# Expert loop: the order of SiLU, gated activations and weight splits

## The chip, the cores and the metric

The kernel runs on one core of one Trainium2 chip. The metric is the device time of one execution in microseconds. Of three executions of the kernel before, the median is 1717.73 us (1715.55 to 1718.81).

## The reference, cut to what matters

The program is one layer of a hybrid backbone: adaLN modulation, a projection, a bidirectional mLSTM and a Fourier group, an output projection, and then a mixture of experts, with float32 throughout. The change touches only the mixture of experts. Each of 1024 tokens goes to 8 of 64 experts; the 8192 assignments are sorted by expert and padded to blocks of 128 rows. For each block:

```python
def expert_block(args):
    xblk, e = args
    g, u = jnp.split(xblk @ w_expert_gu[e], 2, axis=-1)
    return (jax.nn.silu(g) * u) @ w_expert_down[e]
yb = lax.map(expert_block, (xb, block_e)).reshape(n_rows, d)
routed = jax.ops.segment_sum(yb * row_w[:, None].astype(yb.dtype), row_tok, num_segments=n_tok)
```

A block's input is 128 x 1024, the gate-up weights 1024 x 512 (2 MB), the down weights 256 x 1024 (1 MB).

## The kernel before, in words

Five engines run programs of their own and meet at semaphores. The expert loop begins near 670 us and ends near 1662 us; it works on 104 blocks here, two per iteration of the hardware loop, one call of `step` per block on each engine.

A float32 product is made of three fast products: each operand is split in a high part, a rounded copy in a special float32 form, and a low part, the rest. So every weight chunk (128 x 1024; an expert has four gate-up chunks 0 to 3 and two down chunks 4 and 5) is copied by ScalarE (`w_high`, recorded at L742 with all its copies) and then subtracted by VectorE (`w_low`, L2098). ScalarE counts `hi_split`, VectorE `lo_split`. The same is done with the block's transposed rows (`x_high`, `x_low`; L742, L2087) and with its hidden activations (`h_high`, `h_low`; L742, L2091).

TensorE does in step b: eight transposes of block b+1 (L1430), two transposes of the gated activations of block b-1 (`h_transposes`, L1451), the 24 gate-up matmuls of block b (L1443 to L1445), and the 12 down matmuls of block b-1 (L1465 to L1467). The gate-up matmuls wait for one weight chunk every six matmuls (`lo_split`), and the transposes of L1451 wait for `m_hx`, the gated activations.

ScalarE does in step b, in order: `y_evac` (copies the result of block b-2 from PSUM to one of two buffers; it waits until the scatter that last read this buffer is complete), `h_high`, `x_high`, then, if block b has a new expert, that expert's down chunks 4 and 5; then, if block b+1 has a new expert, a wait for its gate-up weights (`gu_ready`) and chunks 0 and 1; then `silu` of block b (L1010; it waits for the gate-up matmuls of block b), and last chunks 2 and 3. VectorE follows the same order: `h_low`, `x_low`, low halves 4 and 5, low halves 0 and 1, `h_rows` (L2105: gated activations, silu(g) * u * row weight), low halves 2 and 3.

SP loads raw weights into two buffers: the gate-up part of expert e (L536) once the low halves of chunks 0 to 3 of expert e-2 are done (`lo_split`), the down part (L539) once chunks 4 and 5 are done. L573 announces landed gate-up weights to ScalarE. GpSimd gathers rows of a later block (index copy L684, gather L687) once `x_low` of an earlier one is done (`m_xb`), and behind that adds a result to the output rows with a scatter (L698); each scatter waits for the one before it.

Of the kernel before, what the change touches and what calls it, by code (L numbers as in the profile page):

```python
# [121 lines left out]
def build(nc, a, out):  # L122

    ctx = ExitStack()
    with ctx:
# [64 lines left out]
        def bank(i):  # L190
            return psum[:, 512 * i:512 * i + 512]
# [145 lines left out]
        def cols(t, o, n):  # L337
            return t[:, o:o + n] if isinstance(o, int) else t[:, bass.ds(o, n)]
# [401 lines left out]
        def _(act):  # L740
            def copy(o, i):
                return act.activation(o, i, ACT.Copy)  # L742
# [108 lines left out]
            def gate_rows(step):  # L851
                if step == 0:
                    act.wait_ge(S("front_dve"), RF_READY)
                    act.activation(Rl, Rf, ACT.Abs).then_inc(S("rl_step"), 1)
                elif step == 1:
                    act.wait_ge(S("rl_step"), 1)
                    act.activation(Rl, Rl, ACT.Exp, scale=-1.0).then_inc(S("rl_step"), 1)
                elif step == 2:
                    act.wait_ge(S("rl_step"), 2)
                    act.activation(Rl, Rl, ACT.Ln, bias=1.0).then_inc(S("rl_step"), 1)  # L860
                else:
                    act.wait_ge(S("front_dve"), W_READY)
                    col_exp(row(1)[64:100], Rw)
                    act.wait_ge(S("front_dve"), E_READY)
                    act.wait_ge(S("rows_exp"), 2)
                    col_exp(row(2)[0:36], Re)
                    act.wait_ge(S("front_dve"), I_READY)
                    act.activation(Ri, Ri, ACT.Exp).then_inc(S("rows_exp"), 1)
# [74 lines left out]
            def w_high(par, chunks):  # L943

                for c in chunks:
                    copy(cols(wsplit, (1 - par) * (2 * WE) + 1024 * c, 1024), cols(raw, (1 - par) * WE + 1024 * c, 1024)).then_inc(S("hi_split"), 1)
# [44 lines left out]
            def x_high(b, p):  # L991

                act.wait_ge(S("m_xt"), b + 1)
                if isinstance(b, int) and b == 1:
                    copy(xTh[p], psY).then_inc(S("m_xh"), 1)
                else:
                    copy(xTh[p], psum[:, 0:1024]).then_inc(S("m_xh"), 1)

            def h_high(b):
                act.wait_ge(S("m_ht"), b + 1)  # L1000
                copy(hTh, bank(7)[:, 0:2 * P]).then_inc(S("m_hh"), 1)

            def y_evac(b, p):
                act.wait_ge(S("block_done"), b + 2)
                act.wait_ge(S(f"added{p}"), 8 * (b - p) + 16)
                copy(yB[:, p], psY).then_inc(S("m_y"), 1)

            def silu(b, p):
                act.wait_ge(S("m_gu"), b + 1)
                act.activation(sg[:, p], bank(3 + p)[:, 0:DE], ACT.Silu).then_inc(S("m_sg"), 1)  # L1010
# [8 lines left out]
            def step(b, p, here, following):  # L1019

                if here is not None:
                    y_evac(b - 2, p)
                h_high(b - 1)
                x_high(b + 1, 1 - p)
                if here is None:
                    act.wait_ge(S("dn_ready"), 2)
                    w_high(1, range(4, 6))
                else:
                    with act.If_ne(act.to_reg(here[0]), 0):
                        act.wait_ge(S("dn_ready"), here[1] + 2)  # L1030
                        act.sem_inc(S("passed"), 1)
                        w_high(1 - (here[1] & 1), range(4, 6))
                first, par1 = following[0], 1 - (following[1] & 1)
                with act.If_ne(act.to_reg(first), 0):
                    act.wait_ge(S("gu_ready"), following[1] + 2)
                    act.sem_inc(S("passed"), 1)
                    w_high(par1, range(2))
                silu(b, p)
                with act.If_ne(act.to_reg(first), 0):
                    w_high(par1, range(2, 4))  # L1040

            def word(b):
                return word_of(act, b)

            step(1, 1, None, fields(word(1)))
            act.wait_ge(S("table_ready"), 2)
            for i in range(2):
                act.wait_ge(S(f"acc_out{i}"), 64)
            rest = act.value_load(pairs_rest[0:1, 0:1], min_val=NE // 2 - 1, max_val=MAXB // 2 - 1)
            with act.Fori(0, rest) as i:  # L1050
                one, two, three = pair_of(act, i)[0:3]
                step(2 * i + 2, 0, one, two)
                step(2 * i + 3, 1, two, three)
# [487 lines left out]
        def _(dve):  # L1541
# [460 lines left out]
            expert, first, ordinal, more_come = trows  # L2002
# [77 lines left out]
            def x_low(b, p, col):  # L2080

                dve.wait_ge(S("m_xh"), b + 1)
                dve.tensor_copy(gcol[:, p:p + 1], xg[:, p, D:XW][:, bass.ds(col, 1)])
                if isinstance(b, int) and b == 1:
                    tt(xTl[p], psY, xTh[p].bitcast(F32), ALU.subtract).then_inc(S("m_xb"), 1)
                else:
                    tt(xTl[p], psum[:, 0:1024], xTh[p].bitcast(F32), ALU.subtract).then_inc(S("m_xb"), 1)  # L2087

            def h_low(b):
                dve.wait_ge(S("m_hh"), b + 1)  # L2090
                tt(hTl, bank(7)[:, 0:2 * P], hTh.bitcast(F32), ALU.subtract).then_inc(S("m_hT"), 1)  # L2091

            def w_low(e, par, chunks):

                for c in chunks:
                    dve.wait_ge(S("hi_split"), 6 * e + (c + 1))
                    high = cols(wsplit, (1 - par) * (2 * WE) + 1024 * c, 1024).bitcast(F32)
                    tt(cols(wsplit, (1 - par) * (2 * WE) + (WE + 1024 * c), 1024), cols(raw, (1 - par) * WE + 1024 * c, 1024), high,  # L2098
                       ALU.subtract).then_inc(S("lo_split"), 1)

            def h_rows(b, p):

                dve.wait_ge(S("m_xb"), b + 1)
                dve.wait_ge(S("m_sg"), b + 1)
                stt(hx[:, p], bank(3 + p)[:, DE:2 * DE], gcol[:, p:p + 1], sg[:, p], ALU.mult, ALU.mult).then_inc(S("m_hx"), 1)  # L2105
# [9 lines left out]
            def step(b, p, here, following, col):  # L2115

                h_low(b - 1)
                x_low(b + 1, 1 - p, col)
                if here is None:
                    w_low(1, 1, range(4, 6))  # L2120
                else:
                    with dve.If_ne(dve.to_reg(here[0]), 0):
                        w_low(here[1] + 1, 1 - (here[1] & 1), range(4, 6))
                first, e1, par1 = following[0], following[1] + 1, 1 - (following[1] & 1)
                with dve.If_ne(dve.to_reg(first), 0):
                    w_low(e1, par1, range(2))
                h_rows(b, p)
                with dve.If_ne(dve.to_reg(first), 0):
                    w_low(e1, par1, range(2, 4))

            step(1, 1, None, fields(word(1)), (word(2) >> 7) & 63)
            dve.wait_ge(S("table_ready"), 2)
            rest = dve.value_load(pairs_rest[0:1, 0:1], min_val=NE // 2 - 1, max_val=MAXB // 2 - 1)
            with dve.Fori(0, rest) as i:
                one, two, three, col3, col4 = pair_of(dve, i)
                step(2 * i + 2, 0, one, two, col3)
                step(2 * i + 3, 1, two, three, col4)
# [88 lines left out]
```

## Time and profile before

| | us |
|---|---|
| median of three executions | 1717.73 |
| profiled execution, its own time | 1716.32 |
| its span | 1714.5 |
| TensorE busy | 1654.9 |
| VectorE busy | 1163.0 |
| ScalarE busy | 838.4 |
| GpSimd busy | 516.3 |

Busy times are sums over the whole span of one profiled execution. Matmuls are pipelined, so a matmul record of 0.39 us overlaps the next one: in the expert loop one starts about every 0.23 us. Helper functions give many operations one line: L742 is every plain copy on ScalarE, told apart by what it writes.

### The profile page before, as it was taken

The page shows a single profiled execution, that of the slowest core. Times are in us where ns is not written, and L with a number is a line of the kernel's source. Part 1 is how long each engine was busy: PE and PEld are TensorE (multiplying, and loading weights), DVE is VectorE, ACT ScalarE, POOL GpSimd, SP SyncE. Part 2 cuts the span into 40 slices and gives each one's busy share as a digit, 9 for nine tenths or more (in the row PEclk, how much of TensorE's full clock was granted, in tenths as well). Part 3 has the DMA queues.
Part 4 walks back from the last instruction along what each step waited for, and adds up shares of the span by engine and source line. Part 5 has one row for each costly group of instructions (what it writes and reads, how often), then busy time and mean ns, then how long its engine had stood idle before and what let it go on. Part 6 is the DMA issues. An engine that isn't in the chain of part 4 may idle for free.

```text
span 1714.5 us, 33430 instructions
## 1 busy us (share of the span) xinstructions
PE 1654.9 (97%) x7875; PEld 1295.6 (76%) x7876; DVE 1163.0 (68%) x1704; ACT 838.4 (49%) x1155; POOL 516.3 (30%) x555
## 2 busy tenths in 40 slices
PE   7999999999999998999999999999999999999997
PEld 1547878879544777888888778888888887888874
DVE  4786895439678697576286887473966796266637
ACT  0323334423310324576286887473865785365624
POOL 2000000026223201343333444433443443343342
PEclk9999999999999999999999999999999999999999
DMA  9740111144353416788688998784988889488764
GB/s 381 273 171 13 38 50 37 52 136 148 148 191 111 172 56 250 236 311 246 171 285 292 339 338 312 224 298 79 363 257 298 267 297 363 83 297 243 224 193 196
DMA packets 98963, 361.65 MB, mean 211 GB/s; under 512 B 19901, under 2 KB 20062, under 8 KB 90469
## 3 DMA queue, kind: packets, MB, share of 16 engines
q1 hardware_dynamic: 68754, 292.29, 44.9%
q0 software_dynamic: 30160, 68.76, 17.8%
q8 instruction: 26, 0.43, 0.1%
q14 instruction: 19, 0.16, 0.0%
q10 hardware_dynamic: 4, 0.02, 0.0%
HBM read 332.66 MB, written 72.72 MB: 236 GB/s over the span
## 4 chain that ended last, share of the span: by engine, by line
PE 75%; DMA 11%; DVE 6%; issue 3%; ACT 2%; SPq 1%; ACTq 1%; DVEq 0%; POOL 0%; POOLq 0%
PE psum L1443 9%; PE psum L1445 9%; PE psum L1444 9%; PE psum L1275 6%; DMA sum_rows<-arena,idxs 6%; PE psum L1467 4%; PE psum L1465 4%; PE psum L1466 4%; PE psum L1430 4%; PE psum L1122 3%; PE psum L1205 3%; PE psum L1206 3%; PE psum L1207 3%; DMA raw_weights<-in_w_gu 3%; DVE arena L1698 2%
## 5 line engine op out<-in xcount | busy, mean ns | idle before, releaser
L2098 DVE TENSOR_TENSOR split_weights<-raw_weights,split_weights (+1 forms) x366 | 428.8, 1221 | 48.5 <-ACT split_weights L742 35.5
L742 ACT ACTIVATE split_weights<-raw_weights (+1 forms) x366 | 364.2, 1060 | 40.8 <-issue 24.9
L742 ACT ACTIVATE arena<-psum 128x1024 f32<-128x1024 f32 (+4 forms) x197 | 157.7, 811 | 418.8 <-DMA sum_rows<-arena,idxs 88.0
L1443 PE MATMUL psum<-split_weights,split_rows 128*128 (+1 forms) x832 | 334.7, 402 | 4.7 <-DVE split_rows L2087 2.3
L1445 PE MATMUL psum<-split_weights,split_rows 128*128 (+1 forms) x832 | 326.8, 393 | 0.0
L1444 PE MATMUL psum<-split_weights,split_rows 128*128 (+1 forms) x832 | 326.6, 393 | 0.0
L698 POOL DMA_INDIRECT sum_rows<-arena,idxs x102 | 172.6, 1692 | 237.4 <-DMA sum_rows<-arena,idxs 197.6
L1443 PEld LDWEIGHTS psum<-split_weights,split_rows 128*128 128x128 f32 x832 | 158.0, 190 | 38.1 <-issue 5.2
L1445 PEld LDWEIGHTS psum<-split_weights,split_rows 128*128 128x128 f32 x832 | 156.9, 189 | 33.3
L684 POOL COPY idxg<-idxT 128x1 uint32 (+1 forms) x107 | 76.1, 711 | 348.8 <-DVE split_rows L2087 276.9
L1444 PEld LDWEIGHTS psum<-split_weights,split_rows 128*128 128x128 f32 x832 | 157.2, 189 | 30.6
L1465 PE MATMUL psum<-split_weights,split_rows 128*128 x416 | 161.9, 389 | 1.5 <-DVE split_rows L2091 1.5
L1467 PE MATMUL psum<-split_weights,split_rows 128*128 x416 | 162.7, 391 | 0.0
L2091 DVE TENSOR_TENSOR split_rows<-psum,split_rows 128x256 fp32r<-128x256 f32 x104 | 43.9, 422 | 174.8 <-ACT split_rows L742 159.8
L1466 PE MATMUL psum<-split_weights,split_rows 128*128 x416 | 161.8, 389 | 0.0
L687 POOL DMA_INDIRECT arena<-t_rows,idxg x107 | 124.5, 1164 | 93.0 <-POOL idxg L684 90.8
L742 ACT ACTIVATE split_rows<-psum 128x256 fp32r<-128x256 f32 (+1 forms) x209 | 136.1, 706 | 7.8 <-PE psum L1451 4.4
L1206 PE MATMUL psum<-u_low,wq_high 128*128 128x512 f32 (+1 forms) x344 | 126.9, 369 | 0.0
L2087 DVE TENSOR_TENSOR split_rows<-psum,split_rows 128x1024 fp32r<-128x1024 f32 x104 | 126.4, 1215 | 0.0
L1010 ACT ACTIVATE arena<-psum 128x256 f32<-128x256 f32 x104 | 39.9, 384 | 175.1 <-PE psum L1445 169.5
L1430 PEld LDWEIGHTS psum<-cst,arena 128*128 128x128 f32 x840 | 110.0, 192 | 10.1 <-DMA arena<-t_rows,idxg 1.2
L1275 PE MATMUL psum<-arena 128*128 128x512 f32 x256 | 112.1, 597 | 1.0 <-DVE arena L1809 0.8
(319 smaller groups left out, 2535.3 us busy)
## 6 DMA issues: line engine op xcount, KB each, us to landing
raw_weights<-in_w_gu SPq DMA_DIRECT2D x62, 2048.0 KB
raw_weights<-in_w_dn SPq DMA_DIRECT2D x62, 1024.0 KB
arena<-in_w_ada SPq DMA_DIRECT2D x12, 2048.0 KB, 8.6
arena<-in_toks SPq DMA_DIRECT2D x18, 512.0 KB, 9.0
extra<-in_w_proj SPq DMA_DIRECT2D x17, 512.0 KB, 3.4
arena<-job_rows SPq DMA_DIRECT2D x16, 512.0 KB, 3.6
arena<-in_w_out SPq DMA_DIRECT2D x2, 2048.0 KB, 9.7
t_rows<-arena SPq DMA_DIRECT2D x8, 512.0 KB, 2.6
```

What stands on the lines that cost most here:

```text
L698: pool.indirect_dma_start(out=y_dram[:, :], out_offset=bass.IndirectOffsetOnAxis(ap=idxs[:, p:p + 1], axis=0), in_=yB[:, p], in_offset=Non ...
L742: return act.activation(o, i, ACT.Copy)
L1206: mm(bank(q % 4)[:, 0:n], wh, u_low[:, k, o:o + n], start=False, stop=False)
L1275: ins = mm(o, mixT[:, k, P * j:P * j + P], wout[:, k, 512 * h:512 * h + 512], start=(k == 4), stop=(k == 3))
L1430: ins = pe.transpose(bank(5 + k // 4 if isinstance(b, int) and b == 1 else k // 4)[:, P * (k % 4):P * (k % 4) + P], xg[:, p, 0:D][:, k::8] ...
L1443: mm(bank(3 + p), xk, part(par, 0, 512 * k), start=(k == 0), stop=False)
L1444: mm(bank(3 + p), xk, part(par, 1, 512 * k), start=False, stop=False)
L1445: ins = mm(bank(3 + p), xl, part(par, 0, 512 * k), start=False, stop=(k == 7))
L1465: mm(bank(first + h), hk, part(par, 0, o), start=(k == 0), stop=False)
L1466: mm(bank(first + h), hk, part(par, 1, o), start=False, stop=False)
L1467: ins = mm(bank(first + h), hl, part(par, 0, o), start=False, stop=(k == 1))
L2098: tt(cols(wsplit, (1 - par) * (2 * WE) + (WE + 1024 * c), 1024), cols(raw, (1 - par) * WE + 1024 * c, 1024), high, ALU.subtract).then_inc( ...
```

## The change

ScalarE no longer splits gate-up chunks 0 and 1 of the next expert ahead of `silu`; it does all four behind it, and the wait for the weights (`gu_ready`) moves behind `silu` too. VectorE makes the low halves of all four behind `h_rows`. Everything else is as it was.

```diff
@@ scalar engine, step(b, p, here, following) @@
                 first, par1 = following[0], 1 - (following[1] & 1)
+                silu(b, p)
                 with act.If_ne(act.to_reg(first), 0):
                     act.wait_ge(S("gu_ready"), following[1] + 2)
                     act.sem_inc(S("passed"), 1)
-                    w_high(par1, range(2))
-                silu(b, p)
-                with act.If_ne(act.to_reg(first), 0):
-                    w_high(par1, range(2, 4))
+                    w_high(par1, range(4))
@@ vector engine, step(b, p, here, following, col) @@
                 first, e1, par1 = following[0], following[1] + 1, 1 - (following[1] & 1)
-                with dve.If_ne(dve.to_reg(first), 0):
-                    w_low(e1, par1, range(2))
                 h_rows(b, p)
                 with dve.If_ne(dve.to_reg(first), 0):
-                    w_low(e1, par1, range(2, 4))
+                    w_low(e1, par1, range(4))
```

## Rows read from the trace of the kernel before

**Rows 1.** The page, part 1: busy time by engine.
```profile
PE 1654.9 (97%) x7875; PEld 1295.6 (76%) x7876; DVE 1163.0 (68%) x1704; ACT 838.4 (49%) x1155; POOL 516.3 (30%) x555
```

**Rows 2.** Timeline of ScalarE, four SiLUs: start, us, engine, line, [idle before].
```profile
686.24 0.39 ACT L1010 ACTIVATE arena<-psum 128x256 f32<-128x256 f32 x1 [2.29 <-PE psum L1445]
863.88 0.38 ACT L1010 ACTIVATE arena<-psum 128x256 f32<-128x256 f32 x1 [2.06 <-PE psum L1445]
1016.23 0.39 ACT L1010 ACTIVATE arena<-psum 128x256 f32<-128x256 f32 x1 [0.24 <-PE psum L1445]
1659.55 0.39 ACT L1010 ACTIVATE arena<-psum 128x256 f32<-128x256 f32 x1 [4.19 <-PE psum L1445]
```

**Rows 3.** Waits in the expert loop: us in total, times, longest.
```profile
PEld psum L1451 <- DVE arena L2105: 11.1, 12, 1.8
ACT arena L742 <- DMA sum_rows<-arena,idxs: 88.0, 35, 5.7
```

**Rows 4.** Chain of waits, 880 to 1060 us: start, us, what.
```profile
884.50 10.30 DMA sum_rows<-arena,idxs
```

**Rows 5.** Timeline of one late step.
```profile
999.32 1.03 ACT L742 ACTIVATE arena<-psum 128x1024 f32<-128x1024 f32 x1 [3.00 <-DMA sum_rows<-arena,idxs]
...
1001.41 3.91 ACT L742 ACTIVATE split_weights<-raw_weights  x4
...
1001.91 1.21 DVE L2087 TENSOR_TENSOR split_rows<-psum,split_rows 128x1024 fp32r<-128x1024 f32 x1
...
1003.13 4.63 DVE L2098 TENSOR_TENSOR split_weights<-raw_weights,split_weights  x4
...
1005.21 0.40 ACT L1010 ACTIVATE arena<-psum 128x256 f32<-128x256 f32 x1
...
1008.83 0.49 PE L1443 MATMUL psum<-split_weights,split_rows 128*128 x1
```

**Rows 6.** Chain of waits, 1281 to 1306 us: a load of gate-up weights.
```profile
1286.85 12.28 DMA raw_weights<-in_w_gu
```

**Rows 7.** Timeline, ScalarE and TensorE in the other late steps.
```profile
1039.17 1.03 ACT L742 ACTIVATE arena<-psum 128x1024 f32<-128x1024 f32 x1 [1.17 <-DMA sum_rows<-arena,idxs]
1044.42 2.01 ACT L742 ACTIVATE split_weights<-raw_weights  x2 [1.14 <-SPq L573]
1227.62 1.03 ACT L742 ACTIVATE arena<-psum 128x1024 f32<-128x1024 f32 x1 [0.88 <-DMA sum_rows<-arena,idxs]
1299.70 2.01 ACT L742 ACTIVATE split_weights<-raw_weights  x2 [1.75 <-SPq L573]
1304.91 0.50 PE L1443 MATMUL psum<-split_weights,split_rows 128*128 x1 [0.22 <-issue]
1423.49 2.01 ACT L742 ACTIVATE split_weights<-raw_weights  x2 [2.36 <-SPq L573]
```

**Rows 8.** Stretches: length, busy PE, PEld, DVE, ACT, POOL; PEclk; DMA share; GB/s.
```profile
882.60:891.90 9.30, 9.30 (x47) 7.88 (x46) 8.97 (x11) 8.40 (x10) 4.09 (x5) 1.00 1.04 369
1003.10:1016.20 13.10, 11.47 (x47) 9.20 (x47) 11.43 (x14) 10.38 (x13) 5.51 (x6) 0.87 0.96 339
```

**Rows 9.** Timeline of undisturbed steps with new experts.
```profile
1131.27 2.01 ACT L742 ACTIVATE split_weights<-raw_weights  x2 [0.68 <-issue]
...
1135.75 1.22 DVE L2087 TENSOR_TENSOR split_rows<-psum,split_rows 128x1024 fp32r<-128x1024 f32 x1
...
1139.55 0.39 ACT L1010 ACTIVATE arena<-psum 128x256 f32<-128x256 f32 x1 [0.38 <-PE psum L1445]
1140.35 2.01 ACT L742 ACTIVATE split_weights<-raw_weights  x2 [0.42 <-issue]
...
1142.05 2.36 DVE L2098 TENSOR_TENSOR split_weights<-raw_weights,split_weights  x2
...
1143.13 0.48 PE L1443 MATMUL psum<-split_weights,split_rows 128*128 x1
```

**Rows 10.** GpSimd's index copies L684 in the loop: duration ns min/median/max, first and last start.
```profile
L684 POOL COPY idxg<-idxT x105: 181/1094/2147, 671.2 to 1657.1; 128x1 uint32 x102, 128x1 uint32<-128x1 uint32 x3
```

## The prediction

> **What bounds the kernel now.** I read the page first: TensorE is busy 97% of the span [rows 1]. So a change off TensorE can only win where TensorE still waits. The edit is in the expert loop, so I asked next how regular that loop is. The SiLU of a block starts some 0.04 us after its gate-up matmuls end; it is the loop's pulse [rows 2]. From 686.24 to 863.88 us lie 19 steps: 177.64 / 19 = 9.35 us, TensorE's own pace. From there 15 steps take 152.35 us (12.1 over 15 x 9.35) and the last 68 take 643.32 (7.5 over). All that can be won in the loop is 12.1 + 7.5 = 19.6 us, or 1.1%.
>
> Then the waits in the loop [rows 3]. TensorE's sequencer waits for VectorE's gated activations (L2105). ScalarE waits 88.0 us for scatters of result rows. The late steps are of two kinds, told apart by the chain of waits.
>
> Kind S, the scatter. From 884.50 to 999 us the chain is nothing but eleven scatter-adds of 8.3 to 10.8 us, one after another, each begun when the one before is done; the first stands for them [rows 4]. ScalarE copies a result out (`y_evac`) only when the scatter two blocks back has landed, and all its later work of the step stands behind. In the worst step [rows 5] `y_evac` starts at 999.32, four splits run without a gap to 1005.3, SiLU starts at 1005.21 though the gate-up ended near 1003.1, VectorE has four low halves ahead of L2105 until 1007.7, and the next gate-up starts at 1008.83: 9.5 us after `y_evac`.
>
> Kind W, the weights. A 2 MB load takes 12.3 us [rows 6]; ScalarE waits for it (SP's announcement, L573), and the next gate-up starts 5.2 us after the first split (1299.70 to 1304.91) [rows 7]. Both kinds come where nearly each block has a new expert and the DMA engines are full: a share of 1.04 at 369 GB/s [rows 8].
>
> **The change part by part.** No instruction is added or removed; work is reordered on ScalarE and VectorE. I replay an undisturbed step that has a new expert before and behind it, SiLU at 1139.55 = 0 [rows 9].
>
> Before: SiLU 0; two splits from 0.80 to 2.8, `y_evac` behind them; the x low half of the step before ends at 1135.75 + 1.22 = 1136.97, that is 6.77 after its SiLU at 1139.55 - 9.35 = 1130.20; low halves of chunks 2 and 3 end at 1144.41 = 4.86 (then SP may load the next gate-up weights into the buffer); the next gate-up starts at 3.58.
>
> After: four splits instead of two between SiLU and `y_evac`: 3.91 us for four in a row [rows 5] from 0.80, so `y_evac` starts at 4.7. From `y_evac` to the end of the x low half it is 3.80 us (999.32 to 1003.12) [rows 5], so that ends at 8.5: 1.75 us later than now. Behind it come two down chunks (2 x 1.16, from the 4.63 us of four) to 10.8, which is 1.5 after the next SiLU, L2105 to 1.9, then gate-up chunk 0 to 3.07 and chunk 3 to 6.57. So: L2105 comes no later than now; gate-up chunk 0 is ready at about 3.1 with some 0.2 of handover, against a need at 3.58 (0.3 spare); each further chunk takes VectorE 1.16 us, and TensorE 6 matmuls of 0.23 = 1.37, so the first decides. The buffer is free at 6.57 instead of 4.86: the gate-up load is issued 1.7 us later. In odd steps the splits start at 1.06 instead of 0.80 (1131.27 - 1130.20) [rows 9], which leaves only 0.05 spare.
>
> Queues: GpSimd's gather of a later block, and behind it the scatter, wait for the x low half, in the code's order; both move 1.75 us later. SP issues the same loads 1.7 us later. TensorE's program is unchanged; its wait for chunk 0 (`lo_split`) was long fulfilled and is now met 0.3 us ahead.
>
> What a late step costs after. Kind S: from `y_evac` 3.80 + 2 x 1.16 + 0.43 (L2105) + 1.17 (chunk 0) + 0.25 = 8.0 us to the gate-up, against 9.5. Kind W: from the first split 1.06 + 1.16 + 0.23 = 2.45, against 5.2. Against this the scatter chain starts 1.75 later and the weights are asked for 1.7 later. If durations of DMAs stay (the engines are full, so a later request is a shift of the whole train), kind S nets 1.75 - 1.5 = +0.25 and kind W 1.7 - 2.75 = -1.05 per place.
>
> The sum by place: the gate-up starts at the latest of natural start, `y_evac` + 1.75 + 8.0, and first split + 1.7 + 2.45; now it is natural start, `y_evac` + 9.5, first split + 5.2 [rows 7]. A natural start is the end of the gate-up before + 3.58, and these ends are the SiLU before + 9.35 (1044.28 is 1016.23 + 3 x 9.35; 1233.07, 1300.30 and 1422.87 are read alike):
> - 864 to 1016 us, one unbroken scatter chain: 12.1 becomes 12.35. +0.25.
> - near 1047: natural 1044.28 + 3.58 = 1047.86; scatter 1039.17 + 9.75 = 1048.92; weights 1044.42 + 4.15 = 1048.57. Late by 1.05, where the two steps now lose 1.7. -0.6.
> - near 1237 and 1247: 1227.62 + 9.75 = 1237.37 against 1236.65, late by 0.7; the second, a first split at 1242.50, comes in time by the same sum as the next line (1246.65 against 1246.7). Now 0.9 + 0.9. -1.1.
> - near 1304: 1299.70 + 4.15 = 1303.85 against 1303.88, in time. Now 1.05. -1.05.
> - near 1428 and 1438: 1423.49 + 4.15 = 1427.64 against 1426.45, 1.2; then the same with a first split at 1433.57: 1437.72 against 1437.0, 0.7. Now 2.9. -1.0.
> - new small waits for chunk 0: 43 steps of the loop carry both a down part and the next gate-up (the four splits in a row of rows 5); 28 of them are outside the late stretches. I take 0.05 us each, the spare of the odd steps being about nil: +1.4. Bounds 0 and 0.3 (0 to 8.4 us).
> - clock: one stretch of the loop runs at a granted 0.87 on average (some 3.4 us at 1.2 instead of 2.4 GHz), behind the 1.5 us gap before L1451 [rows 5, 8]; eight gate-up matmuls take 0.63 instead of 0.39, or 0.2 us more per slot: 1.5 us in all. Other gaps of this size have no such drop. I take no change; bounds -1.5 and +1.5.
>
> Sum: 0.25 - 0.6 - 1.1 - 1.05 - 1.0 + 1.4 = -2.1 us. The profiled execution took 1716.3; 1714.2 after. The median of the runs shown is 1717.7, 1.4 above the profiled one, so I forecast 1715.6 for a median.
>
> A rule that speaks against the change: GpSimd's index copy (L684) takes 181 ns at best, 1094 in the middle and 2147 at most [rows 10], about one or two of VectorE's low halves. The Trainium skill (SBUF — State Buffer, "Who interferes with whom") says that a VectorE instruction with two SBUF inputs and a GpSimd instruction that reads SBUF exclude each other, the later one blocking. That agrees with the steps in that copy's times. By the rule the longer unbroken row of low halves behind the x low half could catch the copy twice instead of once, 2147 - 1094 = 1.05 us more at the head of the scatter chain, and the sum would be -1.05 instead of -2.1.
>
> **The rivals.**
> Full cure: the lateness is ScalarE's and VectorE's order alone, and scatters and loads absorb their later start. For it: SiLU is seen standing behind splits in the late steps. Against: the chain names scatters and loads that take 10 to 12 us, not splits. Then kind S wins 1.5 per first late step and the scatter chain does not move, and kind W wins 2.75: about 10 us, or with every wait gone 19.6. Time 1707 to 1698; I price it at 1708.
> Chunk 0 too late (slower): VectorE now does 4 + 2 low halves, the x halves and L2105 in one unbroken row, about 9.1 of each 9.35 us (busy 8.97 of 9.3) [rows 8], and `y_evac` has lost the idle time it had before it. The point from which it decides: chunk 0's low half ends later than 3.4 us after SiLU. At 0.3 us in 28 steps that is 8.4 instead of 1.4, and a later chain start in the first stretch adds 1: 1715.6 + 8 = 1724. If only half the steps are hit, 1720.
> Nothing moves: the DMA engines' bytes set the end of each crowded stretch, requests and deadlines shift together by the same 1.7 us, and kind W wins nothing either: 1717 to 1718.
>
> **How the numbers follow.** Forecast of a small gain (1713 to 1717): 0.45. Full or half cure: 0.18. Chunk 0 late: 0.20. Nothing moves: 0.17. No change means within 0.2%, 3.4 us, about what a measurement can tell here: 1714.3 to 1721.2. Faster takes all of the cure and some 0.17 of the forecast's 0.45, which lies 1.3 us from the line: 0.35. Slower is the worse half of the late chunk 0 and a little more: 0.20. The rest, 0.45, is no change. The range takes the cure at its price and the late chunk at its worst less a little: 1707 to 1723.
>
> **What would show it.** Right, if in undisturbed steps with two new experts `y_evac` starts 4.7 to 5.0 us after SiLU, the x low half ends near 8.5, the gate-up load is issued 1.7 us later than now, the waits of L1451 for L2105 (11.1 us) are gone and waits of the first L1443 or its load for a low half (L2098) stand in their place, and the stretch 864 to 1016 us is as long as now. Wrong, if that stretch is shorter by more than 2 us (the scatter chain did not bind), if the period of undisturbed steps is above 9.35, or if scatters and loads in the crowded stretches take other times than about 10 and 12 us.

## The result, and the profile after

| | before | after |
|---|---|---|
| median of four executions each, us | 1716.72 (1715.55 to 1718.81) | 1736.34 (1735.52 to 1737.75) |
| profiled execution, its own time | 1716.32 | 1735.52 |
| its span | 1714.5 | 1733.7 |

The changed kernel is slower: ratio 1.0109, 95% interval 1.0097 to 1.0121, some 19.6 us. The forecast of 1715.6 (1707 to 1723) had the wrong sign, and the time lies outside its range. In the code of the changed kernel VectorE's and TensorE's lines stand two lower than before: L2096 is `w_low`, L2103 `h_rows`, L2085 `x_low`, L1449 the two transposes, L1441 to L1443 the gate-up matmuls; ScalarE's L1010 and L742 are unchanged.

The page first, part 1, as in [rows 1]:

```profile
PE 1657.0 (96%) x7875; PEld 1294.5 (75%) x7876; DVE 1152.0 (66%) x1704; ACT 832.8 (48%) x1155; POOL 523.4 (30%) x555
```

The instructions are as many as before and TensorE is busy for almost as long, in a span 19.2 us longer: the added time is waiting. ScalarE's timeline (start, us, engine, line, idle before) has the SiLUs that answer to [rows 2]:

```profile
684.71 0.38 ACT L1010 ACTIVATE arena<-psum 128x256 f32<-128x256 f32 x1 [2.31 <-PE psum L1443]
865.62 0.38 ACT L1010 ACTIVATE arena<-psum 128x256 f32<-128x256 f32 x1 [4.19 <-PE psum L1443]
1019.12 0.38 ACT L1010 ACTIVATE arena<-psum 128x256 f32<-128x256 f32 x1 [1.13 <-PE psum L1443]
1678.68 0.38 ACT L1010 ACTIVATE arena<-psum 128x256 f32<-128x256 f32 x1 [4.19 <-PE psum L1443]
```

With 9.35 us a step, the three pieces of the loop (19, 15 and 68 steps) are late by 3.3, 13.3 and 23.8 us, 40.3 in all, against 0, 12.1 and 7.5 (19.6) before. The crowded stretch is as late as before, but not for the same reason: eight of its 15 steps now have the 0.7 or 0.8 us described below, 6.1 us of the 13.3. The other two pieces were late by 7.5 us before and are by 27.1 now: there the kernel loses its 20 us. Which wait it is, the waits in the loop say (us in total, times, longest), to be read against [rows 3]:

```profile
PE psum L1441 <- DVE split_weights L2096: 24.5, 43, 1.0
PEld psum L1441 <- issue: 32.8, 44, 1.2
PEld psum L1449 <- DVE arena L2103: 1.9, 4, 0.7
ACT arena L742 <- DMA sum_rows<-arena,idxs: 107.5, 31, 7.6
ACT split_weights L742 <- SPq L573: 0.9, 2, 0.7
```

The first matmul of a gate-up (L1441) now waits 43 times for a low half; before, there was no row of this kind. Read step by step, 40 steps of the loop are longer by 0.67 to 0.93 us, 30.8 us together, 0.77 each; all other late steps make 9.8. The row for L1449 has shrunk from 11.1 to 1.9 us, and ScalarE's waits for announced weights (L573) from 14.1 to 0.9: both went as intended. The timeline of one undisturbed step, to be laid beside [rows 9]:

```profile
1137.38 0.38 ACT L1010 ACTIVATE arena<-psum 128x256 f32<-128x256 f32 x1 [1.15 <-PE psum L1443]
...
1138.38 0.47 DVE L2103 SCALAR_TENSOR_TENSOR arena<-psum,gcol,arena 128x256 f32<-128x256 f32 x1
...
1138.55 3.90 ACT L742 ACTIVATE split_weights<-raw_weights  x4 [0.78 <-issue]
...
1140.22 3.50 DVE L2096 TENSOR_TENSOR split_weights<-raw_weights,split_weights  x3 [1.36 <-ACT split_weights L742]
...
1140.80 0.40 PE L1449 MATMUL psum<-cst,arena 128*128 128x128 f32 x2
...
1141.80 0.50 PE L1441 MATMUL psum<-split_weights,split_rows 128*128 x1 [0.60 <-DVE split_weights L2096]
...
1142.36 1.01 ACT L742 ACTIVATE arena<-psum 128x1024 f32<-128x1024 f32 x1
```

VectorE has finished the gated activations at 1138.85 and TensorE its transposes at 1141.20; both then stand still for chunk 0. The chain of waits of the same step (start, us, what; an engine's name with q is its sequencer) shows the way from SiLU to that matmul without a gap:

```profile
1137.38 0.04 ACT arena L1010
...
1138.46 0.04 ACTq L742
1138.50 0.05 issue
1138.55 1.07 ACT split_weights L742
1139.65 0.04 DVEq L2096
...
1140.09 0.08 DVEq L2096
1140.17 0.05 issue
1140.22 1.24 DVE split_weights L2096
1141.46 0.34 issue
1141.80 0.50 PE psum L1441
```

That is 1.17 us from SiLU to the first split (ScalarE's sequencer passes the branch, the weights' wait and the instructions on registers ahead of the split), 1.07 for the split, 0.60 until VectorE starts (the rows DVEq: its sequencer's instructions on registers, run once the split is counted), 1.24 for the low half and 0.34 to the matmul: 4.42 us. TensorE asks at 3.6. The difference is the 0.8 us of an odd step; an even one, whose first split starts at 1.0, loses 0.7.

One thing has to be put right on the code. The branch taken in step b means that block b is the first one of its expert; what is split then, ahead of or behind `silu`, is chunk 0 to 3 of the expert after it (in the same way the down chunks split in step b are those of the expert after block b-1's). So there is a deadline at the very next gate-up only where the expert has a single block. Where it has two or more, the step shows no wait at all (the next gate-up starts 3.58 us after SiLU, as before).

### The profile page after: what moved, and what is told of

Same layout as the page of the kernel before. It is cut to its first block, busy times and chain, and to the rows that moved or that the text cites. A ratio compares the mean times of both kernels' runs of the same rounds, so it can differ in the third digit from the quotient of the medians.

```text
span 1733.7 us, 32168 instructions
## 1 busy us (share of the span) xinstructions
PE 1657.0 (96%) x7875; PEld 1294.5 (75%) x7876; DVE 1152.0 (66%) x1704; ACT 832.8 (48%) x1155; POOL 523.4 (30%) x555
## 4 chain that ended last, share of the span: by engine, by line
PE 65%; DMA 15%; DVE 7%; issue 5%; ACT 4%; ACTq 1%; POOL 1%; SPq 1%; DVEq 1%; POOLq 0%
DMA sum_rows<-arena,idxs 13%; PE psum L1441 8%; PE psum L1443 7%; PE psum L1442 7%; PE psum L1273 6%; PE psum L1120 3%; PE psum L1203 3%; PE psum L1204 3%; PE psum L1205 3%; PE psum L1465 3%; PE psum L1463 3%; PE psum L1464 3%; PE psum L1428 2%; ACT split_weights L742 2%; DVE arena L1696 2%
## 5 line engine op out<-in xcount | busy, mean ns | idle before, releaser
L2096 DVE TENSOR_TENSOR split_weights<-raw_weights,split_weights (+1 forms) x366 | 425.9, 1218 | 78.4 <-ACT split_weights L742 68.2
L742 ACT ACTIVATE split_weights<-raw_weights (+1 forms) x366 | 361.1, 1054 | 38.5 <-issue 37.4
L742 ACT ACTIVATE arena<-psum 128x1024 f32<-128x1024 f32 (+4 forms) x197 | 157.2, 808 | 427.8 <-DMA sum_rows<-arena,idxs 107.5
L1441 PE MATMUL psum<-split_weights,split_rows 128*128 (+1 forms) x832 | 334.7, 402 | 26.9 <-DVE split_weights L2096 24.5
L1443 PE MATMUL psum<-split_weights,split_rows 128*128 (+1 forms) x832 | 325.7, 391 | 0.0
L698 POOL DMA_INDIRECT sum_rows<-arena,idxs x102 | 189.0, 1853 | 222.5 <-DMA sum_rows<-arena,idxs 175.7
L1441 PEld LDWEIGHTS psum<-split_weights,split_rows 128*128 128x128 f32 x832 | 157.2, 189 | 65.4 <-issue 32.8
L684 POOL COPY idxg<-idxT 128x1 uint32 (+1 forms) x107 | 73.3, 685 | 377.0 <-DVE split_rows L2085 305.1
L1443 PEld LDWEIGHTS psum<-split_weights,split_rows 128*128 128x128 f32 x832 | 156.5, 188 | 32.5
L1465 PE MATMUL psum<-split_weights,split_rows 128*128 x416 | 162.7, 391 | 0.0
L687 POOL DMA_INDIRECT arena<-t_rows,idxg x107 | 119.8, 1119 | 93.0 <-POOL idxg L684 90.8
L742 ACT ACTIVATE split_rows<-psum 128x256 fp32r<-128x256 f32 (+1 forms) x209 | 135.5, 703 | 5.6 <-PE psum L1449 4.4
L1010 ACT ACTIVATE arena<-psum 128x256 f32<-128x256 f32 x104 | 40.1, 385 | 195.5 <-PE psum L1443 195.4
L2085 DVE TENSOR_TENSOR split_rows<-psum,split_rows 128x1024 fp32r<-128x1024 f32 x104 | 126.1, 1213 | 0.0
L2103 DVE SCALAR_TENSOR_TENSOR arena<-psum,gcol,arena 128x256 f32<-128x256 f32 x104 | 49.8, 479 | 102.0 <-ACT arena L1010 102.0
```

Of the source, the lines that this page charges most:

```text
L698: pool.indirect_dma_start(out=y_dram[:, :], out_offset=bass.IndirectOffsetOnAxis(ap=idxs[:, p:p + 1], axis=0), in_=yB[:, p], in_offset=Non ...
L1441: mm(bank(3 + p), xk, part(par, 0, 512 * k), start=(k == 0), stop=False)
L1443: ins = mm(bank(3 + p), xl, part(par, 0, 512 * k), start=False, stop=(k == 7))
L1465: ins = mm(bank(first + h), hl, part(par, 0, o), start=False, stop=(k == 1))
```

## The experiments

Two theories are priced in the expectations. The one, H where a letter is used, says that the loss is the wait for chunk 0, since SiLU, one split and one low half in a row do not fit into 3.6 us. Its rival, D, says that it comes from what is released later: results copied out later, so scatters later, and weight buffers freed later, so loads later. "Late time" below is the time of the loop's last SiLU less that of its first, less 102 steps of 9.347 us, in the profiled execution: 19.9 before, 40.6 after.

**One chunk ahead, on both engines.**

```diff
-                    w_high(par1, range(2))
+                    w_high(par1, range(1))
                 silu(b, p)
-                    w_high(par1, range(2, 4))
+                    w_high(par1, range(1, 4))
```

The same with `w_low` around `h_rows`.

> Only gate-up chunk 0 is split ahead of SiLU and of the gated activations, chunks 1 to 3 behind them. Theory H (handover): the added time is the wait of TensorE for chunk 0, 0.69 or 0.83 us in 40 steps (30.8 us), made of ScalarE's and VectorE's address work and semaphore handovers that stand bare behind SiLU. Chunk 0 is then early, chunk 1 needed 1.37 us later, so all 40 waits vanish: 1714 to 1719 us. Theory D (buffers and transfers): the added time comes from weight buffers freed 2.7 us later and scatters 2.1 us later; with one chunk ahead these are still about half as late: 1726 to 1730.

Measured 1717.37 us, ratio to before 1.0005 (0.9995 to 1.0015); late time 18.1. Three of the four chunks still come behind SiLU and the loss is gone. H holds and D's 1726 or more falls: releases later by one chunk (the gate-up load is issued 6.2 us after SiLU in the median, 5.2 before) cost nothing here. Nothing is won either: of the older waits, 14.1 and 8.6 us before, the first grows and the second stands:

```profile
ACT split_weights L742 <- SPq L573: 22.6, 15, 2.8
PE psum L1451 <- DVE arena L2105: 8.4, 10, 1.6
```

**VectorE's half of the change alone.**

```diff
-                with dve.If_ne(dve.to_reg(first), 0):
-                    w_low(e1, par1, range(2))
                 h_rows(b, p)
...
-                    w_low(e1, par1, range(2, 4))
+                    w_low(e1, par1, range(4))
```

> ScalarE as before the change (two chunks ahead of SiLU), VectorE as after (gated activations ahead of all low halves). H: high parts of chunks 0 and 1 are there when VectorE reaches them at about 1.0 us after SiLU, chunk 0 is ready near 2.2 against a need at 3.6, no wait of the 0.7 kind is left: 1712 to 1719 us. D: the buffer is freed 0.9 us later than before, which costs about a third of the 19.6: 1722 to 1726.

Measured 1725.06 us, ratio 1.0050 (1.0033 to 1.0066); late time 29.2. Its waits:

```profile
ACT split_weights L742 <- SPq L573: 56.5, 40, 3.0
PE psum L1443 <- DVE split_weights L2098: 15.4, 14, 1.8
```

H missed here and D's range was hit. ScalarE still asks for the weights ahead of SiLU, but their buffer comes free only when VectorE has made all low halves behind `h_rows`, so the load is mostly issued 6.6 to 7.2 us after the gate-up's end instead of 5.0 to 5.4, and ScalarE waits 56.5 us for weights instead of 14.1. In the undisturbed steps at 1126 and 1135 us the two splits behind that wait end 9.7 us after the last SiLU, so the next SiLU, which is due at 9.35, stands 0.3 us behind them. In the full change ScalarE asks later too, and that wait is 0.9. A late release alone costs less: in "One high part ahead" below the load is issued as late, but one split fewer stands ahead of SiLU and ScalarE asks later by one split. The wait is 24.8 us there and the loss 2 us instead of 8. Which of the two makes the difference was not separated.

**ScalarE's half of the change alone.**

```diff
+                silu(b, p)
                 with act.If_ne(act.to_reg(first), 0):
...
-                    w_high(par1, range(2))
-                silu(b, p)
-                with act.If_ne(act.to_reg(first), 0):
-                    w_high(par1, range(2, 4))
+                    w_high(par1, range(4))
```

> ScalarE as after (SiLU first), VectorE as before (two low halves ahead of the gated activations). H: the low halves wait for ScalarE behind SiLU (start near 2.8 us), so the gated activations end near 5.6 instead of 1.0 to 2.5 and the next gate-up starts near 6.3 instead of 3.6: 2.7 us in each of 59 steps, about 1875 us. D: buffers and scatters are no later than after the change by more than a microsecond, so within 10 us of it: up to 1746.

Measured 1930.67 us, a single execution beside 1716.89 for the kernel before; late time 235.1, or 4.0 us in the mean over 59 steps. VectorE still makes low halves 0 and 1 ahead of `h_rows`, so SiLU's result waits behind splits that come only after it. From its timeline:

```profile
1131.23 0.38 ACT L1010 ACTIVATE arena<-psum 128x256 f32<-128x256 f32 x1 [4.37 <-PE psum L1443]
...
1133.93 2.36 DVE L2096 TENSOR_TENSOR split_weights<-raw_weights,split_weights  x2 [4.79 <-ACT split_weights L742]
...
1136.20 0.48 DVE L2103 SCALAR_TENSOR_TENSOR arena<-psum,gcol,arena 128x256 f32<-128x256 f32 x1
...
1136.74 0.50 PE L1449 MATMUL psum<-cst,arena 128*128 128x128 f32 x2 [1.93 <-DVE arena L2103]
```

The mechanism is the expected one, and it hits each of the 59 steps in which a new expert's weights are split; the size was missed by 55 us. The granted clock is 0.953 in the mean over the span, against 0.993 before. The wait itself is as large as expected, and the clock makes the rest:

```profile
PE psum L1449 <- DVE arena L2103: 118.0, 59, 2.2
```

Two steps with such a gap, from one SiLU to the next (length, busy PE, PEld, DVE, ACT, POOL; PEclk; DMA share; GB/s):

```profile
1304.81:1316.74 11.93, 9.87 (x47) 8.09 (x46) 8.81 (x10) 8.39 (x10) 3.75 (x2) 1.00 0.60 138
1217.23:1230.79 13.56, 11.49 (x47) 9.26 (x46) 8.82 (x10) 8.38 (x10) 4.87 (x4) 0.87 0.71 192
```

TensorE idles 1.9 to 2.2 us before L1449 in each of the 59. Ten of these steps keep the full clock and are late by 2.5 to 2.9 us, 2.7 in the mean, which is the expected figure. In each of the other 49 the granted clock falls once to the level of 1.2 GHz, for 3.4 us, and they are late by 4.2 in the mean. So 59 x 2.7 = 157 us are the wait and 49 x 1.6 = 78 the clock; the 20 us of late steps of the kernel before do not come on top.

**TensorE takes the high weights first.** The changed kernel, in which the 16 products with high weights wait for `hi_split` alone and the 8 with low weights follow:

```diff
-                        pe.wait_ge(S("lo_split"), 6 * e + (k // 2 + 1))
+                        pe.wait_ge(S("hi_split"), 6 * e + (k // 2 + 1))
...
-                    mm(bank(3 + p), xk, part(par, 1, 512 * k), start=False, stop=False)
...
+                for k in range(8):
+                    if k % 2 == 0:
+                        pe.wait_ge(S("lo_split"), 6 * e + (k // 2 + 1))
+                    ins = mm(..., xTh[p][:, P * k:P * k + P], part(par, 1, 512 * k), ...)
```

> The changed kernel with another order of TensorE's gate-up products: all 16 products with the high weights first, waiting for the high parts only, then the 8 with the low weights. Same work. H: high chunk 0 is there at 2.2 us after SiLU, the low ones needed from 7.2 on, so the 40 waits of 0.7 to 0.8 us vanish: 31 us less than after the change, 1703 to 1712 us, below the kernel before. D: nothing of buffers or transfers changes: 1733 to 1738.

Measured 1721.90 us, ratio 1.0030 (1.0020 to 1.0040), so 14.4 us off the changed kernel. No matmul waits for a low half any more; seven waits for a high part are left, 3.2 us in all, and no step of the calm stretches is late by 0.7 or 0.8 us. The rest of the expectation failed: the kernel is 5.0 us slower than the one before, not faster. Late time is 22.6, against 19.9 before, and nearly all of it lies in the crowded stretches, as this wait shows:

```profile
ACT arena L742 <- DMA sum_rows<-arena,idxs: 156.4, 43, 8.3
```

ScalarE waits 156.4 us for scatters, against 88.0 before and 107.5 after. Removing 31 us of waits gave 14. The reading is that the waits had stretched the loop's steps, and that this gave the DMA engines time; what the steps no longer lose, the crowded stretches lose again. The runs with fewer bytes below bear it out: there the same edit gives back 32.1 us.

**Half of the gate-up weights loaded, before and after.** To see the order alone, the DMA load was cut: from the third expert on only 1 MB of the 2 MB of gate-up weights is loaded, and the rest of the product is made from what lies in the buffer.

```diff
-                    load_gu(this, i)
+                    load_gu_half(this, i)
```

> The kernel before, but from the third expert on only the first half of the gate-up weights is loaded (1 MB instead of 2 MB; the other half of the buffer keeps old values). Takes the crowding of the DMA engines away. Theory B (bytes set the late stretches): all 19.6 us of late steps vanish, 1697 us (1695 to 1700). Theory O (order on ScalarE and VectorE sets them): most of them stay, 1708 or more.

> The changed kernel with the same halved gate-up loads. H (handover): the wait for chunk 0 is a fixed latency and does not know of transfers: 0.69 or 0.83 us in each of the 43 or 44 steps followed by a single-block expert's block, 33 to 34 us above half_before, so about 1730 us: the change costs more here than the 19.6 us of full loads, because there part of it hides late steps that came anyway. D (later requests): the cost of the change shrinks with the bytes, 10 us or less above half_before, so at most 1707.

Measured 1696.72 with the old order (ratio 0.9876, 0.9859 to 0.9892) and 1729.93 with the new (1.0069, 1.0052 to 1.0086); late time 0.0 and 33.9. The last SiLU of the loop in each, from ScalarE's timeline, the old order first:

```profile
1639.20 0.38 ACT L1013 ACTIVATE arena<-psum 128x256 f32<-128x256 f32 x1 [4.19 <-PE psum L1448]
```

```profile
1672.99 0.38 ACT L1013 ACTIVATE arena<-psum 128x256 f32<-128x256 f32 x1 [4.19 <-PE psum L1446]
```

And the new order's wait for chunk 0, its line numbers shifted by the added function:

```profile
PE psum L1444 <- DVE split_weights L2099: 23.4, 44, 0.7
```

Two things follow. Late time of the old order needs the bytes: with fewer of them it is nil, in both the scatter and the weight steps, though SiLU still stands behind two splits. And the change alone costs 33.2 us, 44 waits of some 0.76. With all bytes moved some 14 of these 33 fall on time that the crowded stretches lose in either order, and 19.6 are left; the trace of the changed kernel agrees, in which the late time outside those waits is 9.8 us instead of 19.9.

**The same with the high weights first.** Half the gate-up weights, the new order, and TensorE's edit from above.

> high_first with the halved gate-up loads of half_before. H: with transfers out of the way and the low parts needed late, nothing of the change's cost is left: 1697 us, as half_before (1695 to 1699). If something else than the wait for chunk 0 made the change dear (GpSimd's port, VectorE's unbroken row of work), it shows here: 1702 or more.

Measured 1697.83, ratio 0.9870 (0.9847 to 0.9894), late time 2.1: within 1.1 us of the old order. With half the gate-up bytes, then, the waits for chunk 0 are the whole cost of the new order. With all bytes they are 14.4 us of it, and some 5 us stay when they are gone (1721.90 against 1716.89 above). TensorE's edit is not what costs them: below, on top of one chunk ahead, it changes 1717.37 to 1718.20.

**One high part ahead, no low half.** `w_high(par1, range(1))` ahead of `silu` as above, and all four `w_low` behind `h_rows`.

> ScalarE splits chunk 0 ahead of SiLU, VectorE does the gated activations ahead of all low halves. H: the high part of chunk 0 is there when VectorE is done with the gated activations (1.0 to 1.8 us after SiLU), its low half ends near 2.2 to 3.0, in time for 3.6; no waits of the 0.7 kind; the buffer is freed 0.7 to 1 us later than before: 1714 to 1720. D: the later release costs as in vector_only, 1722 to 1726.

Measured 1719.86, ratio 1.0012 (1.0002 to 1.0021), late time 22.4, as expected by H: taking the split out of the row from SiLU to matmul is enough to remove nearly all of the loss. ScalarE waits for weights again (24.8 us), and the matmuls of the crowded stretches for a low half (11.3 us, 10 times); the wait of L1451 stays small (1.3 us).

**One chunk ahead and the high weights first.**

> One chunk ahead of SiLU on both engines, and TensorE takes the products with high weights first. H: one_ahead has no chunk waits left in undisturbed steps, so only late steps can win, some tenths of a microsecond each: 1713 to 1718. D: as one_ahead, 1717.

Measured 1718.20, ratio 1.0003 (0.9993 to 1.0013), late time 19.4. No gain on one chunk ahead alone; H's 1713 to 1718 is missed by 0.2.

**Three chunks ahead.** `range(3)` and `range(3, 4)` on both engines.

> Chunks 0 to 2 ahead of SiLU and gated activations, chunk 3 behind. In steps with down and gate-up splits VectorE reaches the gated activations at 6.8 + 5 x 1.16 = 12.6, that is 3.3 us after SiLU could run; they end at 3.7, the next gate-up starts near 4.3 instead of 3.6: 0.7 us in 43 steps, part of it hidden in late stretches, and scatter-bound steps get worse by 1 us each: 1730 to 1745. If only the number of chunks behind SiLU counted (fewer is better), 1712 to 1717.

Measured 1730.26, ratio 1.0061 (1.0042 to 1.0081), late time 35.8. That is the edge of the expected range: some 40 steps are late by 0.2 to 0.5 us instead of 0.7, 14.8 us together. With 0, 1, 2 and 3 chunks ahead of SiLU the kernel takes 1736.3, 1717.4, 1716.7 and 1730.3 us: a flat bottom between two mechanisms, chunk 0 too late on the one side and on the other SiLU and the gated activations behind too many splits.

**The result copied out later.** Since ScalarE's wait for scatters is the largest wait left, `y_evac(b - 2, p)` was moved from the head of the step to just ahead of `silu(b, p)`, once with one chunk ahead and once in the kernel before.

```diff
-                if here is not None:
-                    y_evac(b - 2, p)
                 h_high(b - 1)
...
+                if here is not None:
+                    y_evac(b - 2, p)
                 silu(b, p)
```

> one_ahead, and ScalarE copies the result of block b-2 out just ahead of SiLU instead of first in the step. A late scatter then holds up neither the x and h copies nor the splits (kind S). If kind S stands on ScalarE's order, about half of the 18 us of late steps go: 1703 to 1712. If the bytes alone set them, 1715 to 1719.

> The kernel before with the same move of the result copy. In steps with four splits in a row ScalarE's work ahead of SiLU ends later by the copy, 1 us: SiLU at 9.9 instead of 9.4, gated activations end near 1.5 to 2.5, still in time for 3.4. Kind S gains as in one_ahead_late_result: 1704 to 1714. If bytes alone set late steps, 1716 to 1722.

Both missed: 1736.19 (ratio 1.0104, 1.0082 to 1.0125) and 1751.55 (1.0188, 1.0164 to 1.0211). The first one's waits:

```profile
PE psum L1465 <- ACT arena L742: 23.4, 24, 3.1
ACT split_rows L742 <- PE psum L1451: 185.0, 79, 3.5
```

The next down matmuls (L1465) write the bank that `y_evac` empties and now wait for it; and ScalarE idles 185 us for the transposes, time in which it had copied the result at no cost. ScalarE's wait for scatters is gone from this trace, and still the kernel is 18.8 us slower than with the copy in its early place. So `y_evac` has to stand early for the sake of the bank that it empties, whatever its wait for the scatter costs there.

No version tried is faster than both kernels. One chunk ahead equals the kernel before.

## Why the prediction was wrong

**The step that failed** is the time of chunk 0: "gate-up chunk 0 is ready at about 3.1 with some 0.2 of handover, against a need at 3.58 (0.3 spare)". It is ready at 4.1 and used at 4.4. Three links were too short:
- The first split was set at 0.80 or 1.06 after SiLU, where it stood as the third of four. As the first it has the weights' wait and its branch ahead of it: 1.0 to 1.17.
- VectorE's start was set by the end of the gated activations, at 1.9. They now end at 1.5, the split at 2.2, and then comes a handover of 0.6 that the sum did not have at all: VectorE starts at 2.84.
- The low half was taken as 1.16, a quarter of four in a row; alone it is 1.22, or 1.24 until it is counted. And from there to the matmul it is 0.34, not 0.2.

The rows on record held the answer. Chunk 2 had in the kernel before the very place that chunk 0 has now, first behind SiLU. In [rows 9] its low half starts at 1142.05 for a SiLU at 1139.55, and ends 3.7 us after it, already later than the need of 3.58. In the odd step it is later still; this row is from VectorE's timeline of the kernel before, for a SiLU at 1130.20 and a split that ended at 1131.27 + 1.06 = 1132.33:

```profile
1132.96 2.36 DVE L2098 TENSOR_TENSOR split_weights<-raw_weights,split_weights  x2 [0.33 <-issue]
```

The first of the two ends near 1134.2, 4.0 after SiLU, and the handover of 0.6 stands bare in it (1132.33 to 1132.96). No matmul waited for chunk 2, so nothing in the waits drew the eye there. The sum put "L2105 to 1.9, then gate-up chunk 0 to 3.07" together from parts where a measured whole stood in the same group. The term of 28 waits of 0.05 us each was therefore 40 steps of 0.77, 30.8 us instead of 1.4, and even its upper bound of 0.3 was under half of one wait.

**The rival that came true** is "Chunk 0 too late", at its own point of decision (later than 3.4 us after SiLU), but for a latency and not, as argued there, because VectorE is full: VectorE stands idle for 1.36 us in front of the low half. It had a chance of 0.20 and a price that ended at 1724. The full cure and the case in which nothing moves are refuted.

**A second step failed, hidden by the first.** The sum had late steps win 3.5 us (0.25 - 0.6 - 1.1 - 1.05 - 1.0). In the changed kernel late time outside the waits for chunk 0 falls by more, from 19.9 to 9.8, but with the waits in place this is no test of it. TensorE taking the high weights first removes the waits and keeps the rest of the change, and then late time is 2.7 us above before and the kernel 5.0 us slower. So, as far as that run stands for it, the forecast would have had the wrong sign with chunk 0 in time too, though inside its range. One part of it is seen: the price of kind W from the first split, 2.45 us, has the same handover missing; the chain above takes 1.07 + 0.60 + 1.24 + 0.34 = 3.25. How the rest divides between scatters that start later and loads that are issued later stays open.

**What was right.** Nothing was added: the instruction counts agree. `y_evac` starts 4.8 to 5.0 after SiLU (forecast 4.7 to 5.0), the x low half ends at 8.9 to 9.0 (8.5), late for the same first split. The gate-up load is issued 2.4 us later where 1.7 was forecast, again by chunk 0's delay. The stretch from 864 to 1016 us takes 153.50 us for its 15 steps, late by 13.3 where 12.35 was forecast and 12.1 before; this is luck, as 6.1 of the 13.3 are waits for chunk 0, and with the high weights first, which has none of them, the same 15 steps are late by 9.3. The scatters of its chain take 7.7 to 11.2 us, as this first one, with the same shape as [rows 4]:

```profile
889.03 11.19 DMA sum_rows<-arena,idxs
```

The weights' waits vanished as the replay of kind W had it. That there was little to win by order is borne out by one chunk ahead, which has no wait for chunk 0 and still equals the kernel before: late time in crowded stretches needs the bytes (0.0 with half the gate-up loads), and none of the orders tried cured it.

**The clock.** The term was taken as nothing. The means are 0.993 before and 0.996 after, and other executions of the kernel before show 0.990 to 0.996, so they do not differ. In the trace the one dip of [rows 8] fell away, 1.5 us by the prediction's price and inside its bounds, while the 43 waits of 0.4 to 1.0 us on TensorE brought none. Of the 59 gaps of 1.9 to 2.2 us in the ScalarE-only kernel 49 were followed by a dip. The ten that were not all come behind a step without such a gap, but so do six of the 49. Why some gaps are followed by a lower clock and others are not stays open.

**The rule of the Trainium skill** that was weighed (SBUF — State Buffer, "Who interferes with whom") could have held the index copy of GpSimd up twice by the longer row of low halves. The trace after does not show it; the row answers to [rows 10] (ns min/median/max):

```profile
L684 POOL COPY idxg<-idxT x104: 182/1005/2142, 671.7 to 1676.2; 128x1 uint32 x102, 128x1 uint32<-128x1 uint32 x2
```

The median is 1005 ns against 1094, and two copies take over 1.5 us against one before, so the extra microsecond did not come. The steps in its times (185 ns, about 1.0 to 1.1 us, 2.1 us) are as before and agree with the rule itself.

## What to carry to other kernels

Before moving work behind an event, write the whole row from that event to the consumer, with a sequencer's gap at every change of engine, and look whether the trace already has an instruction in the place that the moved one will take: its end is the forecast. Work that is split ahead of need should have its first piece, and only its first, ahead of the event; more pieces delay the event, and with none the first piece is late. Here one or two ahead were the same within 1 us, three were worse. Take the bytes away in an experiment to see whether a wait is an order or a load: it turned an argument about 20 us into 33 us of order and 20 us of late time by load, which overlap.

## What the runs showed that was not expected

- A handover from ScalarE to VectorE takes 0.60 us, with the register instructions of VectorE's sequencer inside it, and one from VectorE to a waiting TensorE 0.34 us. From SiLU to a split in a branch behind it, on the same engine, ScalarE takes 1.17 us, of which the SiLU itself is 0.38.
- Waits on TensorE can hide a DMA limit: with 31 us of them removed the kernel gained 14, and ScalarE's wait for scatters rose from 107.5 to 156.4 us. With half the gate-up bytes the same edit gained 32.1.
- A gap of 2 us on TensorE can cost another 1.6 us by the clock: in the ScalarE-only kernel 49 of 59 such gaps were followed by 3.4 us at 1.2 GHz.
- A buffer released 1.6 to 2.1 us later costs 8 us where its consumer asks as early as before (1725.06): ScalarE's waits for weights rise from 14.1 to 56.5 us. Where the consumer asks later too, as in the full change, they fall to 0.9, and with one split fewer ahead of SiLU the same release costs 2 us (1719.86).

Not tried: a VectorE program that has its addresses ready ahead of the wait for the split, which might shorten the 0.60 us.
